# The last tile's expert rows combined on GpSimd, and the last stage's tiles in the order 0, 2, 1

## The reference

```python
gate = jax.nn.softmax(top_val, axis=-1)        # 4 weights of a token
y = sum over its 4 experts of gate[k] * expert_k(h)
x = x + gt * y                                 # gt: 1024 modulation values, of the prompt or of a sample
out = x * rsqrt(mean(x * x) + eps) * g_final
```

## Time and profile before

| | |
|---|---|
| median of 3 runs | 1589.85 us (1587.3 to 1590.73) |
| profiled execution | 1589.99 us |
| its span in the profile | 1587.8 us |
| PE busy | 1505.6 us, 95% |
| DVE / ACT / POOL busy | 34% / 25% / 8% |
| last gather issued | 1565.81 us from the span's start |
| last store issued | 1584.79 us |

### The profile page before, as it was taken

How to read it: one execution, slowest core, us unless ns; L and a number is a source line. 1 busy time by engine, 2 the same in 40 slices (tenths; PEclk the granted TensorE clock), 3 DMA queues, 4 the chain that set the end, 5 groups by cost and what they waited for, 6 DMA issues and landing times.

```text
span 1587.8 us, 29753 instructions
## 1 busy us (share of the span) xinstructions
PE 1505.6 (95%) x12034; PEld 699.1 (44%) x12034; DVE 532.8 (34%) x1105; ACT 391.9 (25%) x784; POOL 129.2 (8%) x196
## 2 busy tenths in 40 slices
PE   7999999998899999999999999999999999999990
PEld 1695445676444344444433434444343444434430
DVE  3412445446622323222232322223232222323225
ACT  1123333411122222222222222222222222222222
POOL 0205021132000000000000000000000000000003
PEclk9999998889699999999999999999999999999995
DMA  9953143112499999999999999999999999999965
GB/s 348 347 203 137 63 163 119 65 35 84 160 338 399 394 383 392 381 375 375 399 382 401 386 378 380 384 392 388 390 387 375 393 372 394 379 398 380 394 232 208
DMA packets 79758, 498.30 MB, mean 314 GB/s; under 512 B 10916, under 2 KB 12308, under 8 KB 26624
## 3 DMA queue, kind: packets, MB, share of 16 engines
q1 hardware_dynamic: 60336, 437.98, 70.8%
q0 software_dynamic: 12048, 38.97, 8.0%
q10 hardware_dynamic: 7344, 20.96, 3.5%
HBM read 475.53 MB, written 23.25 MB: 314 GB/s over the span
## 4 chain that ended last, share of the span: by engine, by line
PE 91%; DVE 4%; DMA 3%; ACT 2%; issue 1%; POOL 0%; SPq 0%; DVEq 0%; ACTq 0%; POOLq 0%
PE ps L1581 43%; PE ps L1586 21%; PE ps L1255 4%; PE ps L1283 4%; PE ps L1483 3%; PE ps L1419 2%; PE ps L1246 2%; PE ps L1381 2%; PE ps L1566 1%; DMA ring<-in_ada_w 1%; PE ps L1440 1%; PE ps L1451 1%; ACT aT L763 1%; PE ps L1435 1%; PE ps L1568 1%
## 5 line engine op out<-in xcount | busy, mean ns | idle before, releaser
L1581 PE MATMUL ps<-ring,xT 128*32 128x512 f32 x4096 | 536.3, 593 | 0.0
L1586 PE MATMUL ps<-ring,xT 128*32 128x512 f32 x2048 | 315.1, 592 | 0.0
L1581 PEld LDWEIGHTS ps<-ring,xT 128*32 128x32 f32 x4096 | 188.5, 110 | 214.5 <-issue 111.5
L1581 PE MATMUL ps<-ring,aT 128*32 128x512 f32 x2048 | 250.8, 595 | 7.6 <-ACT aT L763 7.6
L1149 DVE TENSOR_SCALAR glu<-ps 64x512 f32<-64x512 f32 x64 | 43.7, 682 | 489.0 <-PE ps L1586 489.0
L1586 PEld LDWEIGHTS ps<-ring,xT 128*32 128x32 f32 x2048 | 100.4, 110 | 124.8 <-issue 74.3
L1586 PE MATMUL ps<-ring,aT 128*32 128x512 f32 x1024 | 139.3, 592 | 0.0
L771 ACT COPY half_a<-ps 64x512 f32<-64x512 f32 x64 | 37.3, 582 | 364.6 <-PE ps L1586 364.6
L1581 PEld LDWEIGHTS ps<-ring,aT 128*32 128x32 f32 x2048 | 69.9, 109 | 112.0 <-issue 76.5
L1180 DVE TENSOR_TENSOR y_blk<-ps,half_y 32x512 f32<-32x512 f32 x32 | 21.8, 682 | 270.0 <-ACT half_y L787 270.0
L541 POOL COPY cur_idx<-slot_tok 96x1 int32 (+1 forms) x33 | 6.0, 183 | 1076.0 <-PE ps L1255 1014.7
(11 more groups left out here) (258 smaller groups left out, 1472.2 us busy)
## 6 DMA issues: line engine op xcount, KB each, us to landing
ring<-in_moe_w SPq DMA_DIRECT2D x384, 1024.0 KB, 7.5
ring<-in_ada_w SPq DMA_DIRECT2D x24, 1024.0 KB, 11.6
y_rows<-y_blk ACTq DMA_DIRECT2D x32, 384.0 KB, 7.1
ring<-in_in_w SPq DMA_DIRECT2D x6, 960.0 KB, 14.0
y_rows<-qabs POOLq DMA_DIRECT2D x15, 384.0 KB, 12.4
latT<-in_cache_lat_t POOLq DMA_DIRECT2D x8, 512.0 KB, 3.7
lat<-in_cache_lat POOLq DMA_DIRECT2D x8, 512.0 KB, 4.5
ring<-in_out_w SPq DMA_DIRECT2D x4, 1024.0 KB, 5.6
```

The source lines that it names most:

```text
L1581: nc.tensor.matmul(main[q * SUB:(q + 1) * SUB, :], srcT[:, kt0 + k, g * SUB:(g + 1) * SUB], w[:, k, c, :], start=False, stop=(last and k = ...
L1586: ins = nc.tensor.matmul(extra[q * SUB:(q + 1) * SUB, :], srcT[:, kt0 + k, MAIN:CAP], w[:, k, c, :], start=(first and k == 1), stop=last)
```

## The change

The tiles of the last stage go in the order 0, 2, 1 (`LAST_TILES`), on all engines and in the gathers. Tile 1 (`POOL_TILE`) is no longer combined by DVE, but by POOL, behind its gathers. Since POOL works here from SBUF, ACT first copies the prompt's gates from PSUM into `gates[:, 1, :]`. POOL has no scalar_tensor_tensor in this code: each of the three weighted rows is a tensor_scalar (times the weight, in place) and a tensor_tensor (add), and each instruction waits for the one before. DVE keeps the norm of all three tiles.

```diff
+LAST_TILES = (0, 2, 1)
+POOL_TILE = 1
...
@@ gpsimd
-        for n in range(NT * TOPK):
-            nc.gpsimd.indirect_dma_start(
-                out=y_got[:, n, :], out_offset=None, in_=y_rows,
-                in_offset=bass.IndirectOffsetOnAxis(ap=y_row_idx[:, n:n + 1], axis=0)).then_inc(got_sem[n], 16)
+        for t in LAST_TILES:
+            for n in range(t * TOPK, (t + 1) * TOPK):
+                nc.gpsimd.indirect_dma_start(
...
+        def term(ins):
+            terms[0] += 1
+            ins.then_inc(S["pool_term"], 1)
+            pool.wait_ge(S["pool_term"], terms[0])
+
+        y_acc = y_got[:, POOL_TILE * TOPK, :]
+        pool.wait_ge(S["first_term"], LAST_TILES.index(POOL_TILE) + 1)
+        for k in range(1, TOPK):
+            n = POOL_TILE * TOPK + k
+            pool.wait_ge(got_sem[n], 16)
+            term(nc.gpsimd.tensor_scalar(y_got[:, n, :], y_got[:, n, :], gate_w[:, POOL_TILE, k:k + 1], None, ALU.mult))
+            term(nc.gpsimd.tensor_tensor(y_acc, y_acc, y_got[:, n, :], ALU.add))
+        pool.wait_ge(S["gates_kept"], 1)
+        term(nc.gpsimd.tensor_tensor(y_acc, y_acc, gates[:, 1, :], ALU.mult))
+        nc.gpsimd.tensor_tensor(x[:, POOL_TILE, :], x[:, POOL_TILE, :], y_acc, ALU.add).then_inc(S["pool_x2"], 1)
...
@@ scalar
-        first_term(0)
-        first_term(1)
-        for t in range(NT):
-            a.wait_ge(S["x2_ready"], t + 1)
+        a.wait_ge(S["gates_filled"], 1)
+        nc.scalar.copy(gates[:, 1, :], ps[:, 0:2, :].rearrange("p a b -> p (a b)")).then_inc(S["gates_kept"], 1)
+        for t in LAST_TILES[0:2]:
+            first_term(t)
+        for p, t in enumerate(LAST_TILES):
+            if t == POOL_TILE:
+                a.wait_ge(S["pool_x2"], 1)
+            else:
+                a.wait_ge(S["x2_ready"], p + 1)
...
@@ vector
         combine(0)
-        for t in range(NT):
-            if t + 1 < NT:
-                combine(t + 1)
-            add_eps(t)
-            final_norm(t)
+        for p, t in enumerate(LAST_TILES):
+            if p + 1 < NT and LAST_TILES[p + 1] != POOL_TILE:
+                combine(LAST_TILES[p + 1])
+            add_eps(p, t)
+            final_norm(p, t)
```

More of the change, by code:

```diff
@@ L317, in build @@
             "xT_filled xT_ready gathered idx_ready y_copied y_stored "
-            "first_term x2_ready fin_ss fin_root fin_ready fin_stored gsg_ready pool_gate").split():
+            "first_term x2_ready pool_term pool_x2 gates_kept fin_ss fin_root fin_ready fin_stored gsg_ready pool_gate").split():
         S[name] = sem(name)
@@ L559, in _ @@
         pool.sem_inc(S["pool_gate"], 1)
-        for n in range(NT * TOPK):
-            nc.gpsimd.indirect_dma_start(
-                out=y_got[:, n, :], out_offset=None, in_=y_rows,
-                in_offset=bass.IndirectOffsetOnAxis(ap=y_row_idx[:, n:n + 1], axis=0)).then_inc(got_sem[n], 16)
+        for t in LAST_TILES:
+            for n in range(t * TOPK, (t + 1) * TOPK):
+                nc.gpsimd.indirect_dma_start(
+                    out=y_got[:, n, :], out_offset=None, in_=y_rows,
+                    in_offset=bass.IndirectOffsetOnAxis(ap=y_row_idx[:, n:n + 1], axis=0)).then_inc(got_sem[n], 16)
+        terms = [0]
+        def term(ins):
[12 more added lines that the diff above has]
+        nc.gpsimd.tensor_tensor(x[:, POOL_TILE, :], x[:, POOL_TILE, :], y_acc, ALU.add).then_inc(S["pool_x2"], 1)
         pool.wait_ge(S["out_stored"], 16 * n_out)
@@ L810, in first_term @@
             nc.scalar.activation(rows, rows, ACT.Copy, scale=gate_w[:, t, 0:1]).then_inc(S["first_term"], 1)
-        first_term(0)
-        first_term(1)
-        for t in range(NT):
-            a.wait_ge(S["x2_ready"], t + 1)
+        a.wait_ge(S["gates_filled"], 1)
[7 more added lines that the diff above has]
+                a.wait_ge(S["x2_ready"], p + 1)
             nc.scalar.activation(glu[:, :, :].rearrange("p a b -> p (a b)"), x[:, t, :], ACT.Square, scale=float(D) ** -0.5,
                                  accum_out=stat[:, 56 + t:57 + t]).then_inc(S["fin_ss"], 1)
-            if t + 2 < NT:
-                first_term(t + 2)
-            a.wait_ge(S["fin_ready"], 2 * t + 1)
+            if p + 2 < NT:
+                first_term(LAST_TILES[p + 2])
+            a.wait_ge(S["fin_ready"], 2 * p + 1)
             nc.scalar.activation(stat[:, 59 + t:60 + t], stat[:, 56 + t:57 + t], ACT.Sqrt).then_inc(S["fin_root"], 1)
-            a.wait_ge(S["fin_ready"], 2 * t + 2)
+            a.wait_ge(S["fin_ready"], 2 * p + 2)
             dst = o_yp[0, t * P:(t + 1) * P, :] if t < NP_T else o_ys.rearrange("b q d -> (b q) d")
@@ L1193, in combine @@
             y_acc = y_got[:, t * TOPK, :]
-            v.wait_ge(S["first_term"], t + 1)
+            v.wait_ge(S["first_term"], LAST_TILES.index(t) + 1)
             for k in range(1, TOPK):
@@ L1203, in combine, with final_norm @@
             nc.vector.tensor_tensor(x[:, t, :], x[:, t, :], y_acc, ALU.add).then_inc(S["x2_ready"], 1)
-        def final_norm(t):
-            v.wait_ge(S["x2_ready"], t + 1)
-            v.wait_ge(S["fin_root"], t + 1)
+        def final_norm(p, t):
+            if t == POOL_TILE:
+                v.wait_ge(S["pool_x2"], 1)
+            else:
+                v.wait_ge(S["x2_ready"], p + 1)
+            v.wait_ge(S["fin_root"], p + 1)
             step(nc.vector.reciprocal(stat[:, 48:49], stat[:, 59 + t:60 + t]))
@@ L1210, in final_norm, with add_eps @@
                 S["fin_ready"], 1)
-        def add_eps(t):
-            v.wait_ge(S["fin_ss"], t + 1)
+        def add_eps(p, t):
+            v.wait_ge(S["fin_ss"], p + 1)
             nc.vector.tensor_scalar(stat[:, 56 + t:57 + t], stat[:, 56 + t:57 + t], EPS, None, ALU.add).then_inc(
```

## The result

The changed kernel takes 1601.14 us (median of 11 runs, 1594.82 to 1615.23), the one before 1587.73 (11 runs, 1581.25 to 1591.01): a ratio of 1.0089, with a 95% interval of 1.0064 to 1.0115. It is **slower by 0.9%**, where 0.3% was forecast, and lies above the range given.

A forecast was written before the change was run, and what follows sets the result against it. PE bounds the kernel, but only the last 40 us, ending in a DVE queue, can move. POOL's start 1569.25 + 14.18 + 2.77 of meetings puts the last square at 1586.24 instead of 1581.60: +4.6, 1594.6 us; range 1591.5 to 1598.0.

The forecast's parts named there:

- The engine that ends last: Last stage: the wait before the last square moves from ACT's queue to POOL, which is done at 1586.20 us.
- One tensor input ... so 1.03 us for 1024: POOL's three weighted products in tile 1's combine: priced from cast rows at 1.03 us each, 3.09 together.
- ... and to the end of the span 6.2 us. These 6.2 us stay as they are: From the last tile's square to the span's end: same instructions, so 6.2 us unchanged.
- Two inputs ... 2.12 us for 1024: POOL's five two-input instructions in tile 1's combine: scaled from a 3072-element row to 2.12 us each, 10.60 together.
- That makes three: ... = 2.77 us: DVE and POOL meeting at the shared port: three meetings cost POOL 0.94 + 0.94 + 0.89 = 2.77 us.
- The start: POOL's first instruction, waiting for ACT's third first term and the tenth gather: starts at 1569.25 us.
- The spread: The forecast's own spread around 1594.6 us: -1.5 to +1.7, that is 1593.1 to 1596.3 us.
- POOL isn't held: Rival: only DVE pays at the shared port, so 2.77 us fall away: +1.9, 1591.8 us; chance 0.19.
- as dear as a two-input instruction: Rival: POOL's weighted product costs 2.12 us, not 1.03, adding 3.3 us: 1597.9 us; chance 0.18.
- DVE wasn't starved: Rival: DVE loses every port race, its work standing until POOL ends at 1583.4: near 1598 us; chance 0.03.
- Faster: Rival: POOL's two-input instructions run at a memset's rate, 0.95 us each: -4.2 us, 1585.8 us; chance 0.04.

The follow-up runs named there:

- e3: Changed kernel with a constant 0.25 in place of the weights in POOL's three tensor_scalar: 2.77 us each instead of 2.84, last stage 53.2 us against 53.6.
- e2: Kernel before plus one tiny late POOL copy (128x32) that nothing waits for: last stage 45.6 us against 40.5.
- e5: Kernel before with POOL copies, products and adds appended, alone and beside DVE instructions: for 128x1024, copy 1.03 us, product 2.84, add 2.34.
- e9: Kernel before with six POOL two-input instructions over 32x3072 appended, second input bf16 then f32: 5.98 us with bf16, 6.64 with f32.
- e8: Changed kernel with a plain in-place POOL copy where the three weighted products stand: last stage 48.9 us against 53.6.
- e4: Changed kernel with ACT making all four weighted rows of tile 1, POOL only its five two-input instructions: last stage 46.5 us against 53.6.
- e1: Kernel before with only the tile order changed to 0, 2, 1, DVE combining all three: last stage 41.3 us against 40.5.
- e7: Kernel before with ACT's last square moved earlier, plus POOL multiplying tile 0 by g_final instead of DVE: last stage 40.5 us, 39.7 without the POOL instruction.

## Why the prediction was right and where it was wrong

*The engine that ends last: right.* The stage's end moved from DVE's queue to POOL, the change moved nothing before POOL's start, and the copy of the gates (1.01 us at 1550.75) lay in idle time.

*"One tensor input ... so 1.03 us for 1024": this step failed*, and is the largest miss, 5.45 us. The scaling was sound (a copy takes 1.03), but a product isn't a copy: 2.84 us. The prediction had a rival for it with 0.18, bounded by the price of a two-input instruction; the measured one lies above that bound. The reason it gave, the second operand, is refuted (0.07 us in e3).

*"... and to the end of the span 6.2 us. These 6.2 us stay as they are": this step failed too*, and nothing in the prediction allowed for it. The end of the span is not the last store's landing but the last engine's end, and POOL needs 8.9 us for its drain. In the kernel before that drain was already in the trace, 19 us long, but left out of the views and covered. e2 shows it alone: 4.5 us on the stage for a copy of 0.2 us that nobody waits for. It costs 2.7 us of the 13.1. What makes it 8.9 us long stays open. It isn't the gathers' transfers: in e5 the drain begins 68 us after the last gather's instruction and takes 8.89 us. And it isn't every drain of POOL's: one at the start of the program, behind some memsets of 0.1 us each, took 0.18 us. Every kernel here gives POOL gathers and casts before its end; none was run without.

*"Two inputs ... 2.12 us for 1024": off by 0.22 a piece, 1.09 in all.* The row had a bf16 input (e9). The estimate from the Trainium skill (GPSIMD Engine Reference, Performance versus the Vector engine), 2.25, was nearer than the row; the range's 2.4 held it.

*"That makes three: ... = 2.77 us": one, 1.00 us.* The price of a meeting was right (1.00 here, 0.85 to 0.88 in e8), the count was not. Two of DVE's instructions fell into POOL's products, which let DVE through early (e5), so DVE was held 0.74 and 0.88 us and POOL not at all (2.85 and 2.84, beside 2.84 alone). Had the products been as short as thought, all three would have come, as e8 shows. This miss hid 1.77 us of the others, which was luck. The Trainium skill (SBUF — State Buffer, Who interferes with whom) has the pair of ports held for the whole instruction; copies and sums agree with that (0.08 us), the product doesn't (1.23 of 2.88 us).

*The start, +0.61 us.* The tenth gather landed 6.1 us after its issue and not 5.9, and was issued later, behind a ninth of 1.55 us. That varies from kernel to kernel: 0.94 to 1.98 us for the ninth in the kernels here.

*The spread.* The terms named for it (one meeting of 0.94 less and a start 0.40 earlier; 1.14 a meeting and 2.25 a two-input instruction) add up to -1.3 and +1.3, not -1.5 and +1.7. The range rests on the rivals, so this moved nothing.

*The rivals.* "POOL isn't held" is refuted (1.00 us here, 0.85 to 0.88 in e8). The weighted product "as dear as a two-input instruction" had the right sign and too small a price, 2.12 for 2.84. DVE wasn't starved: its last norm before POOL's x was done at 1579.95, with 13 us of POOL's work to come. "Faster" is refuted too: a two-input instruction takes 2.34 us where it needed under 1.54, and with products made by ACT at no cost to POOL, the stage still loses 6.0 us (e4). Left open: the 0.2 us between the last reciprocal and the last product (1595.08 to 1595.32), which e3, e4 and e8 have too, and e1 and e2 don't.

## What to carry to other kernels

Before work is given to an idle engine at the end of a program, ask when that engine may end: in these kernels POOL's list must be finished some 9 us before the end of the span, so it had no free time at all behind 31 us of the stage. Whether that holds in a program where POOL issues no gathers wasn't tried; the trace's record of the last drain tells. Price an operation from a row of the same operation and the same types, not of the same number of inputs; a small kernel with the operations set out one by one behind the real work gave in one run the prices that the prediction had to guess for copy, product and sum. And work moved from DVE to POOL is paid on DVE too, when DVE has an instruction with two inputs in SBUF to run meanwhile: one POOL instruction of 2.34 us held DVE for 2.15 (e7), and a POOL copy of 1.04 us, with a single input, held it to its end as well (e5).

## What the runs showed that was not expected

- POOL's drain at the end of its list takes 8.9 us after its last instruction, be that a copy of 0.2 us (e2), a chain of sums (the changed kernel, e3, e4, e8: 8.91 to 8.92) or a wait (e5: 8.89); other engines' drains take 0.01 to 1.9 us, their last instruction's own time included.
- POOL's tensor_scalar costs 2.53 ns an element in f32, more than a tensor_tensor (2.10), three times a copy (0.83), and lets DVE's two-input instructions through after 1.23 of its 2.88 us.
- A bf16 second input makes POOL's tensor_tensor of 3072 elements 0.66 us shorter (5.98 against 6.64).
